# Layer 0's first modulation, by blocks of 256 columns: each row of h set and multiplied as its block lands

## The reference, cut to what matters

```
cond = silu(c)
mod = cond @ ada_w[l] + ada_b[l]
sh1, sc1, g1, sh2, sc2, g2 = split(mod, 6)
h = rms_norm(x, mix_norm_g[l]) * (1 + sc1) + sh1
proj = h @ w_in[l]
```

## Time and profile before

| | us |
|---|---|
| median of three runs | 2830.92 |
| lowest, highest | 2830.54, 2833.68 |
| profiled execution, its own time | 2834.17 |
| its span, first to last instruction | 2832.4 |
| PE busy, of the span | 2785.6 (98%) |
| DVE busy | 2493.2 (88%) |
| ACT busy | 1387.9 (49%) |
| POOL busy | 952.5 (34%) |

### The profile page before, as it was taken

How to read it: one execution, slowest core, us unless ns; L and a number is a source line. 1 busy time by engine, 2 the same in 40 slices (tenths; PEclk the granted TensorE clock), 3 DMA queues, 4 the chain that set the end, 5 groups by cost and what they waited for, 6 DMA issues and landing times.

```text
span 2832.4 us, 49104 instructions
## 1 busy us (share of the span) xinstructions
PE 2785.6 (98%) x17864; PEld 2590.7 (91%) x17864; DVE 2493.2 (88%) x5020; ACT 1387.9 (49%) x2321; POOL 952.5 (34%) x773
## 2 busy tenths in 40 slices
PE   7999999999999999999999999999999999999998
PEld 4767789999999999999988788999999999999998
DVE  4667789999999799999987679999999979999998
ACT  3345225477777433333353532445777753333333
POOL 1000018833335244444400000694333434434342
PEclk9999999999999999999999999999999999999999
DMA  7434648999999899999932122699999999999996
GB/s 276 181 119 178 246 157 305 352 337 399 389 382 348 335 387 384 393 390 392 395 119 75 60 74 83 223 345 334 391 386 393 362 335 365 383 386 382 396 387 251
DMA packets 257144, 855.06 MB, mean 302 GB/s; under 512 B 26080, under 2 KB 59104, under 8 KB 250336
## 3 DMA queue, kind: packets, MB, share of 16 engines
q1 hardware_dynamic: 149280, 442.23, 42.1%
q0 software_dynamic: 98496, 381.73, 35.7%
q10 hardware_dynamic: 9216, 29.36, 2.6%
HBM read 777.06 MB, written 76.15 MB: 301 GB/s over the span
## 4 chain that ended last, share of the span: by engine, by line
PE 66%; DVE 19%; DMA 7%; issue 4%; ACT 3%; POOL 1%; SPq 0%; DVEq 0%; ACTq 0%; POOLq 0%
PE banks L1099 32%; PE banks L1636 8%; PE banks L1633 8%; PE banks L1640 8%; DMA w_raw<-wst 5%; PE banks L1597 3%; DVE w_lo L1680 2%; DVE stages L2180 2%; DVE vacc L2192 2%; PE banks L1434 2%; PE banks L1171 1%; ACT w_hi L811 1%; DVE pick L2300 1%; DVE pick L2304 1%; DMA pj<-adaw 1%
## 5 line engine op out<-in xcount | busy, mean ns | idle before, releaser
L811 ACT ACTIVATE w_hi<-w_raw 128x1024 fp32r<-128x1024 f32 x596 | 628.4, 1055 | 632.2 <-PE banks L1099 322.6
L1680 DVE TENSOR_TENSOR w_lo<-w_raw,w_hi 128x1024 fp32r<-128x1024 f32 x522 | 637.8, 1222 | 236.5 <-ACT w_hi L811 192.1
L769 POOL DMA_INDIRECT ring<-v,gidx x320 | 394.1, 1232 | 610.6 <-DVE vacc L2192 520.4
L1099 PE MATMUL banks<-hH,w_hi 128*128 128x352 f32 (+1 forms) x2528 | 513.4, 345 | 2.0 <-ACT act_out L1025 2.0
L1099 PE MATMUL banks<-hH,w_lo 128*128 128x352 f32 (+1 forms) x2528 | 492.2, 336 | 3.2 <-POOL w_lo L756 1.6
L1099 PE MATMUL banks<-hL,w_hi 128*128 128x352 f32 (+1 forms) x2528 | 490.9, 336 | 0.0
L1099 PEld LDWEIGHTS banks<-hH,w_hi 128*128 128x128 f32 x2528 | 415.7, 188 | 39.5 <-issue 11.0
L1099 PEld LDWEIGHTS banks<-hH,w_lo 128*128 128x128 f32 x2528 | 427.0, 188 | 24.9 <-POOL w_lo L756 3.7
L1099 PEld LDWEIGHTS banks<-hL,w_hi 128*128 128x128 f32 x2528 | 427.6, 188 | 19.0
L769 POOL DMA_INDIRECT ring<-u,gidx x244 | 281.8, 1155 | 455.0 <-DVE gact L2180 444.3
L2192 DVE SCALAR_TENSOR_TENSOR vacc<-ring,gcoef,vacc 128x1024 f32<-128x1024 f32 x316 | 404.2, 1279 | 7.1
(11 more groups left out here) (354 smaller groups left out, 3895.9 us busy)
## 6 DMA issues: line engine op xcount, KB each, us to landing
w_raw<-wst SPq DMA_DIRECT2D x596, 512.0 KB, 6.6
activations<-act_out SPq DMA_DIRECT2D x124, 352.0 KB, 8.0
act_in<-activations SPq DMA_DIRECT2D x62, 704.0 KB, 7.3
gate_matrices<-stages ACTq DMA_DIRECT2D x64, 448.0 KB, 7.8
gates<-gate_matrices SPq DMA_DIRECT2D x64, 448.0 KB, 8.9
ada_buf<-adaw POOLq DMA_DIRECT2D x24, 1024.0 KB, 6.9
nrm<-adaw POOLq DMA_DIRECT2D x8, 1024.0 KB, 5.2
pj<-adaw POOLq DMA_DIRECT2D x7, 1024.0 KB, 7.1
```

The costliest lines, as they stand in the source:

```text
L769: pool.indirect_dma_start(out=gather_slot(l, k), out_offset=None, in_=rows[:, :], in_offset=bass.IndirectOffsetOnAxis(ap=gidx[:, k % UG:k ...
L811: nc.scalar.activation(w_hi[g % 2][:, :, :].rearrange("p a b -> p (a b)"), w_raw[:, g % RAWS, :], ACT.Copy).then_inc(s_wh, 1)
L1099: last = mm(bank[s][:, 0:t.stop - t.start], a[s][:, k, :], b[:, k, t], start=(k == 0 and a is w_hi and b is hH), stop=(k == KT - 1 and a i ...
L1680: v.tensor_tensor(w_lo[g % 2][:, :, :].rearrange("p a b -> p (a b)"), w_raw[:, g % RAWS, :], w_hi[g % 2][:, :, :].rearrange("p a b -> p (a ...
```

## The change

In the matrix as it is laid out in HBM, the first eight chunks of layer 0 become eight blocks: block k holds, for all 1024 rows, the 128 shift columns and the 128 scale columns of row k of h. So block k alone is enough to set row k. A block is as large as a chunk (1 MB).

- PE: `first_block(k)` multiplies a block into half of bank 7, eight matmuls of 256 columns in four column groups, halves taken in turn. ACT copies 128x256 sums to `ada_row` (`first_rows`). `first_columns(k)` turns them into two columns of bank 4 with two matmuls of one column. `first_pair(k)` is the part of `project_pair` for row k, six matmuls. In a loop over k, PE runs block k+1, columns k+1, pair k.
- ACT runs `first_rows(k)` between `hH` of row k-1 and `hH` of row k.
- DVE runs for each row in turn `mod`, `gs`, `h32`, and after `hH` the row's `hL`. The constants 1 and sqrt(D) are put into `ada_b` and `g_mix` in advance. `lo(0, 1)` stands between `h32` and `hL` of row 0.
- Loads: x's second half moves from SP to the head of POOL's queue; on SP weight tiles 0 and 1 stand ahead of blocks 1, 3, 5, 7. Blocks are multiplied in the order 0 to 7.
- The `unread` matmuls of layer 0 are placed anew.

```diff
-FIRST_ADA = (0, 2, 1, 4, 3, 6, 5, 7)
-assert sorted(FIRST_ADA) == list(range(KT))
+ADA_BLOCK = ADA_COLS // KT
...
             sp.dma_start(cond[:, :], cT).then_inc(s_cin, 16)
-            for h in range(2):
-                half = slice(h * KT // 2, (h + 1) * KT // 2)
-                sp.dma_start(x[:, half, :], xT[:, half, :]).then_inc(s_in[h], 16)
+            sp.dma_start(x[:, 0:KT // 2, :], xT[:, 0:KT // 2, :]).then_inc(s_in[0], 16)
...
             sp.dma_start(par[:, :], params[0]).then_inc(s_par, 16)
+            load_w(0, 0)
+            load_w(0, 1)
             for k in (1, 3, 5, 7):
                 sp.dma_start(ada_place(k), adaw[0, k]).then_inc(s_ada0[k], 16)
-            load_w(0, 0)
-            load_w(0, 1)
             load_w(0, 2)
             sp.dma_start(fin_g[:, :], final_g).then_inc(s_fgin, 16)
...
+            pool.dma_start(x[:, KT // 2:KT, :], xT[:, KT // 2:KT, :]).then_inc(s_in[1], 16)
             for k in (0, 2, 4, 6):
                 pool.dma_start(ada_place(k), adaw[0, k]).then_inc(s_ada0[k], 16)
...
+            def first_rows(k):
+
+                act.wait_ge(s_adat, k + 1)
+                if k >= 2:
+                    act.wait_ge(s_bmod, k - 1)
+                half = slice(k % 2 * ADA_BLOCK, (k % 2 + 1) * ADA_BLOCK)
+                nc.scalar.activation(ada_row[k % 2][:, 0:ADA_BLOCK], bank[7][:, half],
+                                     ACT.Copy).then_inc(s_brow if k < KT - 1 else s_arow, 1)
...
                 for k in range(KT):
+                    if l == 0 and which == 0 and k >= 1:
+                        first_rows(k)
                     act.wait_ge(s_nrm, l * 2 * KT + (which * KT + k + 1))
                     nc.scalar.activation(hH[:, k, :], h32[:, k, :], ACT.Identity,
                                          bias=mod[:, 3 * which, k:k + 1]).then_inc(s_hh, 1)
...
                 else:
-                    ada_rows(0, 0)
+                    first_rows(0)
                     hi(0, 0)
                     hi(0, 1)
                 normed_hi(l, 0)
...
-                    first, final = 0, KT - 1
-                    if n < KT:
-                        first, final = FIRST_ADA[0], FIRST_ADA[-1]
...
-                                  ada_place(n)[:, j * T:(j + 1) * T], start=(k == first), stop=(k == final))
+                                  ada_place(n)[:, j * T:(j + 1) * T], start=(k == 0), stop=(k == KT - 1))
...
+                def first_block(k):
+
+                    pe.wait_ge(*ada_sem(k))
+                    if k >= 2:
+                        pe.wait_ge(s_brow, k - 1)
+                    for c in range(KT):
+                        last = mm(bank[7][32 * (c % 4):32 * (c % 4) + 32, k % 2 * ADA_BLOCK:(k % 2 + 1) * ADA_BLOCK],
+                                  tiny[:, 0, c:c + 1].broadcast_to([P, 32]),
+                                  ada_place(k)[:, c * ADA_BLOCK:(c + 1) * ADA_BLOCK], start=(c < 4), stop=(c >= 4))
+                    last.then_inc(s_adat, 1)
+
+                def first_columns(k):
+
+                    if k < KT - 1:
+                        pe.wait_ge(s_brow, k + 1)
+                    else:
+                        pe.wait_ge(s_arow, 1)
+                    if k == 0:
+                        pe.wait_ge(s_const, 16)
+                    for m in range(2):
+                        last = mm(bank[4][:, m * KT + k:m * KT + k + 1], ada_row[k % 2][:, m * P:(m + 1) * P],
+                                  dt_sum[:, 0:1], start=True, stop=True)
+                    last.then_inc(s_bmod if k < KT - 1 else s_adam, 1)
+
+                def first_pair(k):
+
+                    if k == 0:
+                        pe.wait_ge(s_wh, 2)
+                        pe.wait_ge(s_wl, 2)
+                        pe.wait_ge(s_taken, 2)
+                    pe.wait_ge(s_rhs, k + 1)
+                    for s in range(2):
+                        for a, b in ((w_hi, hH), (w_hi, hL), (w_lo, hH)):
+                            last = mm(bank[s][:, :], a[s][:, k, :], b[:, k, :],
+                                      start=(k == 0 and a is w_hi and b is hH),
+                                      stop=(k == KT - 1 and a is w_lo))
+                        if k == KT - 1:
+                            last.then_inc(s_tile, 1)
+
                 if l == 0:
-                    for c in FIRST_ADA[0:3]:
-                        ada_chunk(0, c)
                     pe.wait_ge(s_const, 11)
-                norm_groups(2 * l)
-                if l == 0:
-                    ada_chunk(0, FIRST_ADA[3])
-                if l == 0:
-                    for c in FIRST_ADA[4:7]:
-                        ada_chunk(0, c)
-                if l > 0:
+                    unread(10)
+                    norm_groups(0)
+                    unread(4)
+                    first_block(0)
+                    norm_rows(0)
+                    unread(3)
+                    first_columns(0)
                     unread(8)
-                norm_rows(2 * l)
-                if l == 0:
-                    unread(5)
-                    ada_chunk(0, FIRST_ADA[7])
-                    unread(3)
-                    modulation(0, 0, 4)
-                    unread(13)
+                    for k in range(KT):
+                        if k + 1 < KT:
+                            first_block(k + 1)
+                            first_columns(k + 1)
+                        first_pair(k)
+                    ada_chunk(0, KT)
                 else:
+                    norm_groups(2 * l)
+                    unread(8)
+                    norm_rows(2 * l)
                     unread(10)
-
-                project_pair(l, 0, l * RHS_PARTS)
-                if l == 0:
-                    ada_chunk(0, KT)
+                    project_pair(l, 0, l * RHS_PARTS)
...
-                if l == 0 and which == 0:
-                    lo(0, 1)
...
+            def first_modulated():
+
+                ada_b, g_mix = pcol("ada_b"), pcol("g_mix")
+                dve.wait_ge(s_rows, 1)
+                for k in range(KT):
+                    if k < KT - 1:
+                        dve.wait_ge(s_bmod, k + 1)
+                    else:
+                        dve.wait_ge(s_adam, 1)
+                    v.tensor_scalar(mod[:, 0, k:k + 1], bank[4][:, k:k + 1], ada_b[:, k:k + 1], None,
+                                    ALU.add)
+                    link(v.scalar_tensor_tensor(gs[:, 0, k:k + 1], bank[4][:, KT + k:KT + k + 1],
+                                                ada_b[:, KT + k:KT + k + 1], g_mix[:, k:k + 1], ALU.add, ALU.mult))
+                    v.scalar_tensor_tensor(h32[:, k, :], x[:, k, :], gs[:, 0, k:k + 1], bank[2][:, :],
+                                           ALU.mult, ALU.mult).then_inc(s_nrm, 1)
+                    if k == 0:
+                        lo(0, 1)
+                    dve.wait_ge(s_hh, k + 1)
+                    v.scalar_tensor_tensor(hL[:, k, :], h32[:, k, :], mod[:, 0, k:k + 1],
+                                           hH[:, k, :].bitcast(F32), ALU.add, ALU.subtract).then_inc(s_rhs, 1)
...
-                sums = bank[4] if l == 0 else mod_raw
-                link(v.tensor_tensor(m1, sums[:, 0:2 * KT], pcol("ada_b")[:, 0:2 * KT], ALU.add))
+                link(v.tensor_tensor(m1, mod_raw[:, 0:2 * KT], pcol("ada_b")[:, 0:2 * KT], ALU.add))
...
                 if l == 0:
                     padded(0)
+                    scale_b = pcol("ada_b")[:, KT:2 * KT]
+                    v.tensor_scalar(scale_b, scale_b, 1.0, None, ALU.add)
+                    link(v.tensor_scalar(pcol("g_mix"), pcol("g_mix"), float(D) ** 0.5, None, ALU.mult))
                     normed(0)
                     lo(0, 0)
-                    dve.wait_ge(s_adam, 1)
-                    first_modulation(0)
+                    first_modulated()
                 else:
                     normed(2 * l)
                     lo(l, 1)
-                modulated(l, 0)
+                    modulated(l, 0)
...
     ada = a["ada_w"].reshape(L, KT, P, ADA_SETS, ADA_COLS).transpose(0, 3, 1, 2, 4).reshape(L, ADA_CHUNKS, P, ADA_COLS)
+    ada[0, 0:KT] = a["ada_w"][0][:, 0:ADA_COLS].reshape(KT, P, 2, KT, P).transpose(3, 1, 0, 2, 4).reshape(KT, P, ADA_COLS)
```

More of the change, by code:

```diff
@@ L492, in build @@
         s_adam = sem("modulation_done")
+        s_brow = sem("first_rows_of_block_taken")
+        s_bmod = sem("first_modulation_of_block_done")
         s_modr = sem("next_modulation_taken")
```

## The result

The changed kernel takes 2838.56 us (median of 11 runs, 2836.42 to 2844.10); the kernel before, run beside it as often, 2832.46 us (2830.54 to 2836.34). The ratio is 1.0022 with a 95% interval of 1.0014 to 1.0029: slower by some 6 us, where a gain of 0.2 us was forecast. The profiled execution took 2839.88 us, its span 2838.1.

A forecast was written before the change was run, and what follows sets the result against it. PE was taken as the bound, 98% busy, with layer 0's stage ending at the eighth h32 row: block 1 at 22.1, 1.6, six 3.4 us laps, row done 45.8 against 46.0. So 2830.92 - 0.2 = 2830.7 us, range 2827.0 to 2834.0.

The forecast's parts named there:

- block 1 lands and is begun: Layer 0 loads on SP's queue: block 1 was taken to land at 22.1 us, between 21.8 and 22.3.
- block 1, copy, handovers: Between block 1's landing and columns 1: block 1.05, ACT's copy 0.43, handovers 0.12, together 1.6 us.
- first lap: First of six PE round trips from columns 1 at 23.7 us to columns 7, claimed at 3.4 us.
- five more laps: The rest of the six PE round trips up to columns 7 at 44.1 us, each claimed at 3.4 us.
- columns 7 to the end of the row: Columns 0.6, two small operations 0.35, row 0.74 us: eighth h32 row done at 45.8 us.
- chunk 8 and a tile at full clock: After the eighth h32 row: POOL's chunk comes at 51.3 us, and nothing after it is changed.
- I keep the full clock, from the row with the nearest wait: PE in layer 0's loop: clock stays full through waits, as after 2.37 us idle at 1588.7 us.
- Rival 2: PE drops to 1.2 GHz waiting for block 1; laps grow about 2.7 us, total 2848.2 us; chance 0.07.
- 128 more of POOL's 8 KB packets: Extra POOL packets passing before block 1 on SP's queue: 1.05 MB, costing 2.4 us at 430 GB/s.
- The lap: PE's round trip per row: pair 1.37, block 1.05, copy 0.43, handovers 0.12, columns 0.45; 3.4 us, ends 3.0 to 4.4.
- Rival 1: Queues share by bytes, block 1 there by 17 us, first pair about 21.1; 3.0 us better, 2827.7; chance 0.10.
- Rival 3: A block's narrow matmuls bound by weight loads, 1.90 instead of 1.05 us, seven times; 2836.4 us; chance 0.08.

The follow-up runs named there:

- another order of the loads: Changed kernel with POOL's queue carrying blocks 0, 1, 3, 5 and SP's 2, 4, 6, 7; ratio to the kernel before 1.0000, median 2834.51 us.
- the turned loop: Changed kernel with columns 1 ahead of the loop, then PE running block k+2, pair k, columns k+2 per lap; ratio to the kernel before 1.0004, 2836.92 us.
- the last kernel: Changed kernel with reordered block loads, turned loop and early chunk 8 load, plus 7 unread matmuls before block 2; ratio to the kernel before 0.9969, 2826.39 us.
- the loads as they were: Changed kernel with the earlier loads: both x halves on SP, weight tiles 0 and 1 behind the chunks; ratio to the kernel before 1.0057, 2850.38 us.
- the three edits together: Changed kernel with reordered block loads, PE's turned loop and chunk 8's load waiting only for the root's rows; ratio to the kernel before 0.9969, 2827.45 us.

## Why the prediction was wrong

The path was right, and most prices were. Of the 7.9 us between the forecast of 2830.7 and the measured 2838.56, 1.5 are the kernel before, whose median beside it was 2832.46 and not 2830.92; the rest, some 6 us, is the change. The eighth `h32` row was forecast at 45.8 us and is done at 51.0; chunk 8 follows it by 0.29 + 5.20 us of load, as forecast. Term by term, up to the start of chunk 9 (its 6.7 is what the kernel before took, since nothing behind chunk 8 was to change):

| step | forecast | measured | late by |
|---|---|---|---|
| block 1 lands and is begun | 22.1 | 23.4 | 1.3 |
| block 1, copy, handovers | 1.6 | 2.44 | 0.8 |
| first lap | 3.4 | 5.39 | 2.0 |
| five more laps | 17.0 | 18.0 | 1.0 |
| columns 7 to the end of the row | 1.7 | 1.79 | 0.1 |
| chunk 8 and a tile at full clock | 6.7 | 8.27 | 1.6 |

These make 6.8 us; the forecast gain of 0.2 taken off, 6.6, the 6.62 us by which chunk 9 is late.

**The step that failed** is the sentence "I keep the full clock, from the row with the nearest wait". The row showed a clock of 1.00 over one wait of 2.37 us. The wait for block 1 became 3.43 us, and the clock fell at 23 us, when block 1 should have been at work since 22.1; whether it would have stayed up with the block on time no run shows. Moreover the row was one sample: in the changed kernel the very same wait in layer 1, again 2.37 us, was followed by 0.66 (the last stretch shown of it), and the eight matmuls after it took 3.95 us instead of 2.42. The three rows of the table that hold the clock (0.8, 2.0, 1.6) make 4.4 us (0.2 of the first lap's 2.0 are the lap itself, below); filling the waits took back 4.1. The second fall, at chunk 8, was not in the forecast at all, though the wait of 2.4 us was, to a tenth. Rival 2 had the mechanism and a price per lap of 2.7 (2.0 were measured, the clock coming back within the first lap), but was given 0.07; the forecast gain being 0.2 us, one such fall was enough to turn the sign. The Trainium skill (TensorE: Matmul & The Clock Gate, "Loop structure matters more than you think") says that PE goes cold in a loop that has a long wait for a transfer between its matmuls. The trace of the changed kernel agrees for the wait (0.50 from 23.0 us), but not with the sum that the prediction drew from it: from 29.8 us on the laps had brought the clock back to 1.00.

**Block 1** was late by 1.3 us. The packets alternate as forecast, 191 on POOL's queue and 188 on SP's from 10 to 15 us:

```profile
q0 software_dynamic: 191, 1.43, 67.8%
q1 hardware_dynamic: 188, 0.70, 34.4%
```

The landing lies past the end of the range given for it (21.8 to 22.3). The term that was too small is "128 more of POOL's 8 KB packets": up to the landing of block 1 at 23.36 us POOL's queue passed 638 packets, 161 more than the 477 up to that of chunk 1 before (19.87), and all queues together moved 1.38 MB more, not 1.05. Why 161 and not 128 was not tried.

**The lap** was 3.60, not 3.4: from the first matmul of a pair to the block 1.57 us passed, not 1.37. The copy (0.39), the block (1.04), the columns and DVE's way were right. The experiment with the turned loop shows that the 0.5 us of idle time in it was the round trip named in the forecast.

**Rival 1**, block 1 at 17 us if queues share by bytes, is refuted by the packet counts. Its price was near: with block 1 at 17 by another order of the loads, the first pair began at 21.7, where the rival had 21.1. **Rival 3** is refuted: blocks took 1.07 us in every lap at full clock. Its sum has a slip, which changes nothing: 5.9 us more than 2830.7 are 2836.6, not 2836.4.

**The range** was too narrow because a fall of the clock was bounded by one slow lap in part, in one place; it fell in two places of the stage.

## What to carry to other kernels

A loop that paces itself by loads and round trips needs its idle time looked at twice: once as time, once as what PE's clock does afterwards, and one profile is too little for the second. Matmuls that nobody reads can fill such a wait; 26 more of them took back 4.1 us of this stage. Order blocks on the queues by when they are needed, counting packets and not bytes. Before a loop is made serial, put the engine's next independent work (here the pair) between the two halves of its round trip.

## What the runs showed that was not expected

The clock's fall after a short wait is not the same from run to run of like code. After the wait of 2.37 us in layer 1 it stayed at 1.00 in the profiles of the kernel before and of four experiments; it fell in those of the changed kernel and of the other four, and each of these lost 1.3 to 1.5 us there. The profiled execution of the last kernel, with the 7 `unread` more, shows it:

```profile
1585.00:1590.00 5.00, 5.00 (x41) 3.25 (x41) 3.10 (x4) 3.29 (x5) 0.00 (x0) 0.66 0.00 0
```

The wait before chunk 8 is as varied: of the four profiles that have it at over 2 us the clock fell in two (2.36 us in the changed kernel, 2.25 with the loads as they were) and stayed in two (2.25 with the other order of the blocks, 2.33 with the turned loop). What decides it was not found.

Nor does it take one long wait: with the three edits together it fell around two pauses of 0.50 and 1.37 us, and with the order of the loads alone, where a pair fills the second pause, it did not.

Early in the program the clock column is no guide: in the kernel before it reads 1.00 in every 5 us stretch from 10 to 25 us, while a chunk takes 1.93 us there (at 19.89), as long as block 1 of the changed kernel at a granted 0.50.
